# The opening of a one-core inference step: modulation vectors in two halves, and eighteen products that nobody reads

## The reference

```
mod = silu(cond) @ w_ada + b_ada                 # 1024 x 6144, for two conditions
sh1, sc1, g1, sh2, sc2, g2 = split(mod, 6)
h = rmsnorm(x, norm1_g) * (1 + sc1) + sh1
proj = h @ w_in                                  # 1024 x 1440: u, v, pooling, c_q, c_kv, k_rope
... gated MLP, pooling mixer, latent attention -> @ w_out
x = x + g1 * mix
h = rmsnorm(x, norm2_g) * (1 + sc2) + sh2
x = x + g2 * experts(h)                          # 16 experts, each takes its best 128 + 16 tokens
y = rmsnorm(x, final_norm_g)
```

## Time and profile before

| | us |
|---|---|
| median of three executions | 1600.95 |
| the profiled execution | 1600.96 |
| its span, first to last instruction | 1598.8 |
| TensorE busy in the span | 1551.1 (97%) |
| VectorE busy | 562.4 (35%) |
| ScalarE busy | 420.2 (26%) |

### The profile page before, as it was taken

How to read it: one execution, slowest core, us unless ns; L and a number is a source line. 1 busy time by engine, 2 the same in 40 slices (tenths; PEclk the granted TensorE clock), 3 DMA queues, 4 the chain that set the end, 5 groups by cost and what they waited for, 6 DMA issues and landing times.

```text
span 1598.8 us, 26689 instructions
## 1 busy us (share of the span) xinstructions
PE 1551.1 (97%) x10773; PEld 1249.3 (78%) x10773; DVE 562.4 (35%) x1343; ACT 420.2 (26%) x958; POOL 105.7 (7%) x108
## 2 busy tenths in 40 slices
PE   5999999999999999999799999999999999999997
PEld 3744545766766666544599999999999999999996
DVE  2201545765656574126674111111111111111114
ACT  4300112555545453234311111101111111111114
POOL 0005300000000000111000000000000000000000
PEclk9999999999999999999899999999999999999999
DMA  9780002000010300352476787778787787877776
GB/s 381 271 292 33 30 7 59 8 20 8 0 26 0 125 1 1 129 187 80 185 269 234 277 312 252 268 274 306 268 296 266 266 299 267 310 252 270 270 235 248
DMA packets 120922, 291.06 MB, mean 182 GB/s; under 512 B 17503, under 2 KB 21126, under 8 KB 117918
## 3 DMA queue, kind: packets, MB, share of 16 engines
q1 hardware_dynamic: 115534, 270.80, 46.7%
q0 software_dynamic: 4752, 17.30, 4.1%
q10 hardware_dynamic: 576, 2.10, 0.3%
HBM read 266.18 MB, written 21.64 MB: 180 GB/s over the span
## 4 chain that ended last, share of the span: by engine, by line
PE 93%; DVE 3%; DMA 2%; ACT 1%; issue 1%; SPq 0%; DVEq 0%; POOLq 0%; ACTq 0%
PE ps L1163 31%; PE ps L1192 16%; PE ps L805 9%; PE ps L601 9%; PE ps L906 7%; PE ps L854 5%; PE ps L839 4%; PE ps L671 2%; PE ps L759 2%; DMA wreg<-in_w_ada_dram 1%; PE ps L771 1%; PE ps L784 1%; PE ps L621 1%; PE ps L1112 1%; PE ps L1120 1%
## 5 line engine op out<-in xcount | busy, mean ns | idle before, releaser
L1163 PE MATMUL ps<-mreg,wreg 128*128 128x144 f32 x4096 | 517.1, 286 | 1.4 <-ACT hreg L1455 1.4
L1163 PEld LDWEIGHTS ps<-mreg,wreg 128*128 128x128 f32 x4096 | 508.8, 190 | 1.8 <-ACT hreg L1455 1.6
L1192 PE MATMUL ps<-mreg,wreg 128*128 128x144 f32 x2048 | 267.3, 287 | 0.5 <-DVE mreg L2118 0.5
L1192 PEld LDWEIGHTS ps<-mreg,wreg 128*128 128x128 f32 x2048 | 259.5, 191 | 0.7 <-DVE mreg L2118 0.7
L2105 DVE TENSOR_TENSOR mreg<-ps,mreg 128x144 f32<-128x144 f32 x120 | 36.9, 307 | 434.2 <-PE ps L1163 434.1
L805 PE MATMUL ps<-wreg 128*128 128x512 f32 (+2 forms) x400 | 171.7, 519 | 0.2
L1483 ACT ACTIVATE mreg<-ps 128x144 f32<-128x144 f32 x128 | 37.1, 290 | 444.7 <-PE ps L1163 444.7
L601 PE MATMUL ps<-hreg,wreg 128*128 128x512 f32 (+1 forms) x432 | 142.9, 489 | 0.0
L906 PE MATMUL ps<-wreg,mreg 128*128 128x512 f32 x288 | 130.8, 598 | 0.0
L839 PEld LDWEIGHTS ps<-const,hreg 128*128 128x128 f32 x648 | 79.9, 141 | 58.8 <-issue 39.3
L601 PEld LDWEIGHTS ps<-hreg,wreg 128*128 128x128 f32 x432 | 70.5, 191 | 69.7 <-issue 69.4
(11 more groups left out here) (280 smaller groups left out, 1124.5 us busy)
## 6 DMA issues: line engine op xcount, KB each, us to landing
wreg<-in_w_e_dram SPq DMA_DIRECT2D x96, 2048.0 KB, 12.0
wreg<-in_w_ada_dram SPq DMA_DIRECT2D x24, 1024.0 KB, 10.0
out_dram<-wreg SPq DMA_DIRECT2D x9, 512.0 KB, 2.6
wreg<-in_x_sample_dram SPq DMA_DIRECT2D x8, 512.0 KB, 5.0
wreg<-in_w_out_dram SPq DMA_DIRECT2D x1, 4096.0 KB, 12.8
x_rows<-wreg SPq DMA_DIRECT2D x8, 512.0 KB, 4.2
xn_rows<-wreg SPq DMA_DIRECT2D x8, 512.0 KB, 2.6
wreg<-x_rows SPq DMA_DIRECT2D x8, 512.0 KB, 9.3
```

The source lines that it names most:

```text
L1163: mm = pe.matmul(o[:, 0:CAP], w[s][:, k, (f % 4) * P:(f % 4 + 1) * P], xsT[b][:, k, :], start=(k == 0), stop=(k == KD - 1))
L1192: mm = pe.matmul(bank[4 + dm % 2][:, 0:CAP], w2[f // 4][:, f % 4, dm * P:(dm + 1) * P], hidT[:, f, :], start=(f == 0), stop=(f == 7))
```

## The change

The modulation for group 0 is computed in two halves of the features, and the first products run on the first half while the second is loaded.

- `w_ada`'s first 8 MB come as eight rounds of 1 MB, each of two DMAs of 512 KB: rounds 0 to 3 hold the columns for shift and scale of k0 to k3, rounds 4 to 7 those of k4 to k7. Each round has two of the eight row blocks, on two pairs of quadrants of the output.
- `mod 0` and `mod 1` are products with a 4-column selector (`mod_sel`) that also adds the two pairs; they were four transposes before. The former `ada 1`, `ada 2` are now `ada 2`, `ada 3`.
- On TensorE: after `vecs`, 18 products of the identity with itself into the bank that `ada 0` then overwrites; transposes of k0 to k3, rounds 0 to 3, transposes of k4 and k5, `mod 0`, transposes of k6 and k7; then the first half (k0 to k3) of `va` 0 to 3 and of `u 0 0`, `u 1 0`, with rounds 4 to 7 in between; `mod 1`; the second half of the same products; then the transposes of the other groups as before.
- x2 and x3 are loaded on SyncE's queue, ahead of the vectors. `w_in` comes as u and v columns of k0 to k3, the same of k4 to k7, and the rest in one piece that waits for nothing. The later `ada` chunks use six places in turn.
- VectorE modulates k0, k2, k3 and later k4, k6, k7; ScalarE k1 and later k5, and only then takes the squares of x4 to x8.

TensorE's list from its second instruction to the transposes of the later groups, before: the names after the arrow are the operands' regions (`mreg` the rows, `cond` the conditions, `rt` the modulation rows, `hreg` is `hT`).

The core of the diff:

```diff
+ADA_ROUNDS = (range(0, 4), range(4, 8), range(8, 16), range(16, 24))
-    jobs = [("vecs", "D")] + rows[0] + [("ada", 0, "D"), ("mod", 0, "D")]
-    jobs += [("va", t, "A") for t in range(4)] + rows[1] + rows[2]
...
+    jobs = [("vecs", "D")] + rows[0][0:4] + [("ada", 0, "D")] + rows[0][4:6] + [("mod", 0, "D")] + rows[0][6:8]
+    jobs += [("ada", 1, "D"), ("mod", 1, "D")] + [("va", t, "A") for t in range(4)]
+    jobs += [("u", 0, 0, "A"), ("u", 1, 0, "A")] + rows[1] + rows[2]
...
+                if n >= RING:
+                    sp.wait_ge(ada_mm, n - RING + 1)
+                slot = ada_ring[n % RING]
+                if n < KD:
+                    half, q = divmod(n, 4)
+                    places = slot.rearrange("p (j s f) -> p j s f", j=2, s=2)
+                    for j in range(2):
+                        k = 2 * q + j
+                        src = w_ada[0, k * P:(k + 1) * P, 0:2048].rearrange("p (s x) -> p s x", s=2)
+                        sp.dma_start(places[:, j, :, :], src[:, :, half * 512:half * 512 + 512]).then_inc(ada_in[n % RING], 16)
...
+            def first_products():
+                pe.wait_ge(w_in_in[0], 16)
+                for t in range(4):
+                    evicted(pe, BEFORE[NUM[("va", t)]])
+                    va_part(t, range(0, 4))
+                    if t % 2:
+                        ada_part(1, range(4 + t // 2, 5 + t // 2))
+                evicted(pe, BEFORE[NUM[("u", 0, 0)]])
+                u_part(0, range(0, 4))
+                ada_part(1, range(6, 8))
+                evicted(pe, BEFORE[NUM[("u", 1, 0)]])
+                u_part(1, range(0, 2))
...
                     mm = pe.transpose(o[:, 0:V_ROWS], vecs[0:V_ROWS, :], ident[0:V_ROWS, 0:V_ROWS])
+                    unread_products(BANK[NUM[("ada", 0)]], 18)
...
+                        if job[1] < 2:
+                            mm = pe.matmul(o[:, 4 * j:4 * j + 4], columns, mod_sel, start=True, stop=True)
...
-            for t in range(4):
+            for t in range(2):
                 act.dma_start(x_sb[t], tok_rows(x_sample, x_prompt, t)).then_inc(rows_landed[t], 16)
...
-                        for k in D_MODULATES:
+                        for k in D_MODULATES[3 * r:3 * r + 3]:
+                            evicted(dve, NUM[("h", 0, k)])
```

More of the change, by code:

```diff
@@ L385, in build, with ada_there @@
         LATE, PROMPT = 8, 9
-        def ring_slot(n):
-            return n if n < RING else (n - KD) % RING
+        def ada_there(n):
+            return sum(32 if m < KD else 16 for m in range(n % RING, n + 1, RING))
         def evicted(eng, n):
@@ L422, in ada_chunk @@
             def ada_chunk(n):
[L424 to L433, removed]
+                if n >= RING:
[8 more added lines that the diff above has]
+                        sp.dma_start(places[:, j, :, :], src[:, :, half * 512:half * 512 + 512]).then_inc(ada_in[n % RING], 16)
+                else:
+                    r, k = divmod(n, KD)
+                    sp.dma_start(slot, w_ada[0, k * P:(k + 1) * P, r * 2048:(r + 1) * 2048]).then_inc(ada_in[n % RING], 16)
             def w_in_part(s):
[L436 to L439, removed]
+                k0, kn, a, z = ((0, 4, 0, OFF_P), (4, 4, 0, OFF_P), (0, KD, OFF_P, COLS))[s]
+                sp.dma_start(w_in_sb[:, k0:k0 + kn, a:z],
+                             w_in[0, k0 * P:(k0 + kn) * P, a:z].rearrange("(k p) f -> p k f", p=P)).then_inc(w_in_in[s], 16)
+            for n in range(4):
                 ada_chunk(n)
@@ L596, in _, with unread_products @@
         def _(pe):
+            def unread_products(b, n):
+                for _ in range(n):
+                    pe.matmul(bank[b][:, 0:P], ident, ident, start=True, stop=True)
             def project(n, w_at, m, g):
@@ L603, in project, with ada_part @@
                 return mm
-            def ada_part(r, ks):
-                o = bank[BANK[NUM[("ada", r)]]]
+            def ada_part(part, rounds):
+                o = bank[BANK[NUM[("ada", part)]]]
+                first, last = ADA_ROUNDS[part][0], ADA_ROUNDS[part][-1]
                 pe.wait_ge(cond_ok, 1)
-                for k in ks:
[L611 to L623, removed]
+                for n in rounds:
+                    pe.wait_ge(ada_in[n % RING], ada_there(n))
+                    for g in range(4):
+                        k = 2 * (n % 4) + g // 2 if n < KD else n % KD
+                        mm = pe.matmul(o[32 * g:32 * g + 32, :], cond[:, k, :], ada_ring[n % RING][:, g * 512:(g + 1) * 512],
+                                       start=(n == first), stop=(n == last))
+                    mm.then_inc(ada_mm, 1)
@@ L627, in _ @@
                 o = bank[BANK[n]]
[L629 to L632, removed]
+                ahead = {("va", 6): 2, ("u", 1, 1): 3}.get(job[:-1], 0)
+                if ahead:
+                    evicted(pe, BEFORE[NUM[("ada", ahead)]])
+                    ada_part(ahead, ADA_ROUNDS[ahead][0:4])
                 if BEFORE[n] >= 0:
@@ L666, in _ @@
                         evicted(pe, NUM[("h", t // 4, KD - 1)])
[L667 to L672, removed]
+                    mm = va_part(t, range(4 if t < 4 else 0, KD))
                 elif kind == "u":
-                    pe.wait_ge(w_in_in[1], 16)
-                    mm = project(n, 0, job[1], job[2])
+                    mm = project(n, 0, job[1], job[2]) if job[2] else u_part(job[1], range(4, KD))
                 elif kind == "pin":
@@ L746, in _ @@
                     mm.then_inc(job_mm, 1)
+                if job[:2] == ("mod", 1):
+                    u_part(1, range(2, 4))
             last = len(JOBS) - 1
```

114 lines of the change are left out of this document (72 added, 42 removed).

## The result

The changed kernel takes 1623.3 us (median of 4 executions, 1622.28 to 1624.62); the kernel before took 1602.58 beside it (4 executions, 1598.79 to 1604.91). The ratio is 1.0132, with an interval of 1.0112 to 1.0152: it is slower by 1.3%, where 1594.5 was forecast. The profiled spans say the same, 1598.8 before and 1621.7 after, 22.9 us more.

What follows compares the result with a forecast made beforehand. TensorE bounds the kernel, waiting first for the eighth `w_ada` chunk. Later transposes at 56.4 against an equal point of 63.2 gain 6.8, less 0.3 for small waits: 1600.96 - 6.5 = 1594.5 us; range 1592 to 1599 with partial cases and scatter.

Steps and rivals of the forecast that it cites:

- The step that failed: After the opening: the remaining work is unchanged, so the opening's gain, 6.8 us less 0.3, stays to the end.
- The rival that ended slower: Opening: TensorE stays at 1.2 GHz until the dense work, costing 11.6 us: 1606; chance 0.08, including 0.02 for 512 KB pieces.
- Products: Opening, before the first transposes: unread products take 5.8 us, 7.6 at the lower clock, and buy the upper clock.
- First half: Opening: 16 transposes to 17.3, four rounds to 20.7, bias to 21.4, `mod 0` 0.9 to 22.3.
- the sign named for it: Opening: first-half rounds ending after 22 us, because products and transposes ran at 0.21, would show the forecast wrong.
- Start of `va`: End of the first-half modulation: TensorE begins `va` at 23.5 and is dense from about 24.7, after waiting for ScalarE's k1.
- Dense work to the later transposes: From 24.7: `va` products 13.4, rounds 4 to 7 3.57, two `u` jobs 13.8, `mod 1` 0.9; together 31.7, ending 56.4.
- What must be there in time: Opening loads: first `w_in` piece at 22.9, needed 23.5; rounds 6 and 7 at 32.6, needed 37; biases just in time.
- the gap: Near 23 us: late `w_in` or biases (1 to 2 us) or a clock fall (1.9) leave gain 2.5 to 4.5: 1597.5; chance 0.13.
- SyncE's queue: Opening loads: SyncE holds until four rounds land, `w_in` comes at 25.5, dense work at 26.5; gain 4, 1597; chance 0.09.
- The clock from 24 to 40: Start of dense work: TensorE's granted clock is 1.00 from 24 to 40 us; the clock gives 1.9 us of the gain.
- Hole before the later transposes: Late x4 to x8 squares make TensorE wait 2 to 4 us near the opening's end: 1597.5; a rival, chance 0.08.

Runs made afterwards that it cites:

- 36 instructions on: Changed kernel without its 18 unread products, with 24 met waits (12 instructions) heading TensorE's list: 1596.62 us, one run.
- 48 instructions on: Changed kernel without its 18 unread products, with 48 met waits (24 instructions) heading TensorE's list: 1633.82 us, one run.
- 60: Changed kernel with 9 unread products of 256 columns in place of 18 of 128: 1633.66 us, ratio 1.0209.
- 96 on: Changed kernel, 1623.3 us; kernel before with 192 met waits added, 1632.68; changed kernel with 144 met waits in place of the unread products, 1622.03.

## Why the prediction was wrong, step by step

**The step that failed:** "After the opening the same work stands in the list, so the gain stays." The same work does stand there, but not in the same place. The change puts 96 instructions ahead of it, and the loop's body is then fetched again at every jump back: 27 us, against a gain of 4. I had laid out the opening on every engine and queue, and passed over what the trace of the kernel before could have told me: the instruction queue's 44 packets, and that none of them falls between 1050 and 1500 us, when the loop is past its first turn. A turn there (97.65 us from one jump to the next) has 800 passes, as many loads and 66 other instructions, 1666 in all by a count of the trace, which were plainly not fetched in each turn; I didn't ask what kept them.

None of the rivals was this either. The rival that ended slower put the loss into the opening, with the clock that does not rise. The clock did fall, at a price of 10.5 us in all, but as a consequence of waits at 1040 us and later.

The Trainium skill (Runtime: NRT & Kernel Launch, section Instruction fetch mechanics) says that code comes in blocks of 16 KiB, 256 instructions, and that TensorE's memory holds 2048. The packets of 16 KB agree. The same section says that a taken branch to a target outside the current window of two pages forces a fetch before execution goes on. The trace agrees that there is such a wait, 2.9 to 3.7 us here; it does not agree on the window, since a body of some 1600 instructions came through 450 us of turns with no packet at all.

With blocks of that size a picture fits every row of the table: the body is a little over six blocks long, lies on seven or on eight of them by where it starts, and is kept only if it lies on seven; 128 instructions fewer make it seven almost anywhere, 120 more make it eight. The list has a second long loop, in the attention, of 1423 instructions and three turns; a body of that length lies on six or seven blocks, and between 385 and 550 us, in its later turns, no run has an instruction packet, wherever it begins. The 9 packets of a turn are one more than the eight blocks of the picture; what the ninth is isn't shown. What is shown is that place and length decide, that the loss comes and goes with 45 packets, and that the edge is between 36 and 48 instructions on. Where the blocks begin isn't shown, so the picture is argued from the pattern. Open too is why the wait is longer near the edge (24.6 and 24.4 at 48 and 60) than at 96 on (16.0 to 16.6).

**The terms of the opening.**

- *Products:* 5.8 us taken, between 3.9 and 7.6; they took 7.12, 0.2 a pass, so by their durations nearly all of them ran at the lower level (the clock column has 1.00 there, as it had in the stretch from 16 in the earlier trace rows). They ended at 16.95, not at 15.5. That they buy the clock was right (16 transposes in 1.75, and 3.68 without); that it pays isn't shown.
- *First half:* rounds' end 20.7 forecast (the terms add to 20.9), 22.26 measured, late by the products' 1.4; so the sign named for it, an end after 22, was there. `mod 0` 0.9 forecast, 0.91 measured, but from 23.29 and not from 21.4: the transposes of k4 and k5, 1.02, outlasted the bias.
- *Start of `va`:* 23.5 and dense from 24.7 forecast, 25.47 and 26.51 measured. The wait for ScalarE's tile is there, but short: 0.38 of TensorE, at the end of the 0.81 that ScalarE takes for the tile.
- *Dense work to the later transposes:* 31.7 forecast, 32.7 measured (26.51 to 59.23).
- *What must be there in time:* right. TensorE has no wait on `w_in`, the biases or the second half before the later transposes, and the DMA share is 1.03 to 1.06 in the stretches shown. So neither the gap nor SyncE's queue cost anything.
- *The clock from 24 to 40:* right, 1.00 where it was 0.74 and 0.84.
- *Hole before the later transposes:* none, as forecast.

With these terms the opening gains 4.0 to 4.4 instead of 6.8. A gain of about that size shows once the loop is whole: the kernel without the products is 5.0 us shorter in its span than before.

## What to carry to other kernels

A loop with a long body (1666 instructions here) is part of every edit ahead of it: compare the instruction queue's packets of both profiles and look for "issue" at the head of the loop before explaining anything else, and compare edits of the opening with the loop held in one place. Unread products, waits and other padding are not free when they lengthen a list; here 18 of them brought nothing that the traces show where they stand, and cost 27 us a thousand microseconds later. In this kernel 72 instructions fewer ahead of the loop, 160 more, or a body 128 shorter (with work left out) each took the loss away whole.

## What the runs showed of the hardware

- A jump back costs either nothing or a wait of 2.9 to 5.1 us and, after it, 1.6 to 3.3 us in the first 32 passes, since TensorE comes back at its lower level (granted 0.50 from 1044 to 1046). Nothing lies between: 36 instructions on there are 44 packets as before, 48 on there are 89.
- A block that is fetched again has no long price in transfers (0.64 MB in 450 us): the loss is the wait, not the bandwidth.
- A wait that is met already is not free. With 96 instructions of two such waits at the start of its list TensorE began its first transpose at 11.28 us, with 160 at 18.17, about 0.11 us for each (64 more, 6.89 us); 60 of them in the loop left a gap of 4.74, 0.08 for each.
